# Rotary lanes 32 partitions apart, exchanged by ScalarE copies instead of permutation products

## The reference, cut to what matters

```
xr = x[..., :ROT_DIM]; x1, x2 = xr[..., :half], xr[..., half:]      # ROT_DIM 16, half 8
rot = concatenate([x1 * cos - x2 * sin, x2 * cos + x1 * sin])
x = concatenate([rot, x[..., ROT_DIM:]])
```

## Time and profile before

| | us |
|---|---|
| median of 3 runs | 2611.5 (2610.76 to 2611.63) |
| the profiled execution, its own time | 2610.73 |
| its span in the profile | 2608.9 |
| TensorE busy | 2572.1 (99%) |
| VectorE busy | 1674.5 (64%) |
| ScalarE busy | 1380.8 (53%) |
| granted TensorE clock, mean | 0.998 |

### The profile page before, as it was taken

How to read it: one execution, slowest core, us unless ns; L and a number is a source line. 1 busy time by engine, 2 the same in 40 slices (tenths; PEclk the granted TensorE clock), 3 DMA queues, 4 the chain that set the end, 5 groups by cost and what they waited for, 6 DMA issues and landing times.

```text
span 2608.9 us, 38082 instructions
## 1 busy us (share of the span) xinstructions
PE 2572.1 (99%) x14854; PEld 2228.0 (85%) x14854; DVE 1674.5 (64%) x1827; ACT 1380.8 (53%) x1640; POOL 61.1 (2%) x30
## 2 busy tenths in 40 slices
PE   8999999999999999999999999999999999999998
PEld 7888898888888988888888888888888888898887
DVE  7766687556765666666666666666766666665665
ACT  6644565445545664454455544544654454465544
POOL 0000000001000000000000000000000000000000
PEclk9999999999999999999999999999999999999999
DMA  7455534554554345555543455454345555543551
GB/s 272 144 196 191 181 138 178 193 191 173 196 192 178 130 148 191 193 177 193 193 146 117 176 192 193 178 193 177 130 154 193 185 185 186 186 161 114 194 193 65
DMA packets 63496, 454.36 MB, mean 174 GB/s; under 512 B 7088, under 2 KB 7344, under 8 KB 8992
## 3 DMA queue, kind: packets, MB, share of 16 engines
q1 hardware_dynamic: 62064, 449.15, 48.0%
q0 software_dynamic: 896, 3.05, 0.4%
q10 hardware_dynamic: 432, 0.68, 0.1%
HBM read 451.79 MB, written 1.05 MB: 174 GB/s over the span
## 4 chain that ended last, share of the span: by engine, by line
PE 92%; DVE 4%; ACT 3%; issue 1%; DMA 0%; ACTq 0%; DVEq 0%
PE tb L489 28%; PE tb L494 14%; PE acc L287 10%; PE acc L288 10%; PE acc L289 10%; PE acc L253 2%; PE acc L255 2%; PE acc L256 2%; PE acc L897 1%; DVE w_lo L211 1%; PE acc L489 1%; PE acc L899 1%; PE acc L898 1%; PE tb L318 1%; ACT w_hi L204 1%
## 5 line engine op out<-in xcount | busy, mean ns | idle before, releaser
L211 DVE TENSOR_TENSOR w_lo<-raw,w_hi 128x2048 fp32r<-128x2048 f32 x416 | 952.6, 2293 | 314.7 <-ACT w_hi L204 314.5
L204 ACT ACTIVATE w_hi<-raw 128x2048 fp32r<-128x2048 f32 x425 | 812.9, 1914 | 314.4 <-PE acc L289 276.5
L489 PE MATMUL tb<-xT,w_hi 128*128 128x512 f32 x3168 | 792.0, 392 | 0.0
L489 PEld LDWEIGHTS tb<-xT,w_hi 128*128 128x128 f32 x3168 | 576.3, 188 | 108.5 <-DVE big L682 0.2
L494 PEld LDWEIGHTS tb<-xT,w_lo 128*128 128x128 f32 x3168 | 432.1, 190 | 31.0
L494 PE MATMUL tb<-xT,w_lo 128*128 128x256 f32 x3168 | 441.7, 282 | 0.0
L287 PE MATMUL acc<-w_hi,cat 128*128 128x512 f32 x1024 | 402.8, 393 | 3.5 <-DVE cat L582 3.5
L288 PE MATMUL acc<-w_hi,cat 128*128 128x512 f32 x1024 | 399.9, 390 | 0.0
L289 PE MATMUL acc<-w_lo,cat 128*128 128x512 f32 x1024 | 398.7, 389 | 0.0
L287 PEld LDWEIGHTS acc<-w_hi,cat 128*128 128x128 f32 x1024 | 192.7, 188 | 42.8 <-DVE cat L582 3.9
L289 PEld LDWEIGHTS acc<-w_lo,cat 128*128 128x128 f32 x1024 | 192.3, 188 | 41.1
(11 more groups left out here) (349 smaller groups left out, 2882.7 us busy)
## 6 DMA issues: line engine op xcount, KB each, us to landing
raw<-in_stream SPq DMA_DIRECT2D x425, 1024.0 KB, 4.8
h<-in_x SPq DMA_DIRECT2D x2, 512.0 KB, 5.9
xn<-in_gates POOLq DMA_DIRECT2D x2, 512.0 KB, 8.0
gain<-in_gains POOLq DMA_DIRECT2D x2, 512.0 KB, 5.3
out<-xn SPq DMA_DIRECT2D x2, 512.0 KB, 2.9
cst<-in_consts SPq DMA_DIRECT2D x1, 832.0 KB, 12.6
raw<-in_stream ACTq DMA_DIRECT2D x1, 512.0 KB, 8.3
raw<-in_stream SPq DMA_DIRECT2D x1, 512.0 KB, 9.1
```

What stands on the lines that cost most here:

```text
L204: act.activation(w_hi[:, k % SPLIT, :], raw[:, k % RAW, :], ACT.Copy).then_inc(hi_done, 1)
L211: dve.tensor_tensor(w_lo[:, k % SPLIT, :], raw[:, k % RAW, :], w_hi[:, k % SPLIT, :], ALU.subtract).then_inc(lo_done, 1)
L489: return pe.matmul(bank, w_hi[:, c % SPLIT, at:at + P], xT[:, kt, :, :].rearrange("p a t -> p (a t)"), start=first, stop=last)
```

## The change

- The host reorders the columns of the q and k weights (`partners_apart`): in each 64 lanes the second eight rotary lanes change places with lanes 32 to 39. Partners then lie 32 partitions apart. The sign of the sine goes into the table rows.
- The matrix `rot` and its 16 products are gone. The constants' two DMAs are cut at the next boundary and carry 64 KB less in all.
- ScalarE does not copy the whole bank as it is, but with four activations of 32 partitions x 512 columns each, from partitions 32.. to 0.., 0.. to 32.., 96.. to 64.., 64.. to 96.. (`shift`), into one of two buffers `partner`, which lie in `gain`, not used at that time. Before it reuses a buffer it waits for `turned` of the tile that used it last.
- These copies stand behind the split of the same point of ScalarE's queue, not ahead of it. In `qkv_act` and `mix_a_act` the same change of order is made.
- VectorE multiplies the bank itself with the cosine, the partner buffer with the sine, and adds. It waits for `shifted`. In `qkv_dve` the split of chunk 4 moves between the two first turns.
- In `plan` the entries "rotate" are now "turn", so the cut in steps of 24 is unchanged; TensorE skips them.

```diff
-                        seq.append(("rotate", e - 1))
+                        seq.append(("turn", e - 1))
-            def rotate(self, e):
-                self.pe.wait_ge(*when("copied", (self.i, e)))
-                self.pe.matmul(fed_bank(e), rot, q_or_k(e), start=True, stop=True)\
-                    .then_inc(*sig("rotated", (self.i, e)))
...
                 for unit in units:
-                    {"product": self.product, "rotate": self.rotate, "block": self.block}[unit[0]](*unit[1:])
+                    if unit[0] != "turn":
+                        {"product": self.product, "block": self.block}[unit[0]](*unit[1:])
...
+        def shift(act, dst, bank, done):
+            for a in range(0, P, HD):
+                for to, of in ((a, a + HD // 2), (a + HD // 2, a)):
+                    last = act.activation(dst[to:to + HD // 2, :], bank[of:of + HD // 2, :], ACT.Copy)
+            last.then_inc(*sig("shifted", done))
...
-        def copy_act(act, i, c, e):
+        def shift_act(act, i, c, e):
             used(act, c + e)
-            act.activation(q_or_k(e), fed_bank(e), ACT.Copy).then_inc(*sig("copied", (i, e)))
+            if e >= 3:
+                act.wait_ge(*when("turned", (i, e - 3)))
+            shift(act, partner[e % 3], fed_bank(e), (i, e))
...
-            b, r = two(q_or_k(e)), two(rot_a)
+            b, r = two(q_or_k(e)), two(partner[e % 3])
-            dve.wait_ge(*when("rotated", (i, e)))
-            if e:
-                dve.wait_ge(*when("turned", (i, e - (1 if e % 3 == 1 else 2))))
-            dve.tensor_tensor(r, two(fed_bank(e)), sin, ALU.mult)
-            dve.tensor_tensor(b, b, cos, ALU.mult).then_inc(*sig("own", ("turn", i, e)))
+            dve.wait_ge(*when("shifted", (i, e)))
+            dve.tensor_tensor(b, two(fed_bank(e)), cos, ALU.mult)
+            dve.tensor_tensor(r, r, sin, ALU.mult).then_inc(*sig("own", ("turn", i, e)))
             dve.wait_ge(*when("own", ("turn", i, e)))
             dve.tensor_tensor(b, b, r, ALU.add).then_inc(*sig("turned", (i, e)))
...
                         v_take(act, i, c, unit[1])
-                    elif kind == "moba":
-                        copy_act(act, i, c, unit[1])
                     split_hi(act, c, unit[1] + SPLIT)
+                    if kind == "moba" and unit[1] % 3 != 2:
+                        shift_act(act, i, c, unit[1])
...
         def qkv_act(act, kind, i, c, n):
-            if kind == "moba":
-                copy_act(act, i, c, 0)
             split_hi(act, c, SPLIT)
             if kind == "moba":
-                copy_act(act, i, c, 1)
+                shift_act(act, i, c, 0)
             split_hi(act, c, 1 + SPLIT)
+            if kind == "moba":
+                shift_act(act, i, c, 1)
...
                 split_lo(dve, c, SPLIT)
-                turn_dve(dve, i, 0)
-                turn_dve(dve, i, 1)
+                turn_dve(dve, i, c, 0)
+                split_lo(dve, c, 1 + SPLIT)
+                turn_dve(dve, i, c, 1)
...
-            product(K0, {7: lambda: rotate(Q0)})
+            product(K0)
...
-            rotate(K0)
             product(G1)
...
-            product(K1, {3: lambda: rotate(Q1)})
-            value(V0, {4: lambda: rotate(K1)})
+            product(K1)
+            value(V0)
...
-            raw_copy(Q0)
             split_hi(act, c, Q0 + SPLIT)
-            raw_copy(K0)
+            apart(Q0)
             split_hi(act, c, K0 + SPLIT)
+            apart(K0)
...
-            raw_copy(Q1)
+            apart(Q1)
...
             exps(1)
-            raw_copy(K1)
+            apart(K1)
             split_hi(act, c, Q1 + SPLIT)
             flip_copy(0)
             split_hi(act, c, K1 + SPLIT)
             values(V0)
...
+def partners_apart(w):
+    at, half_ = np.arange(HD), HD // 8
+    at[half_:2 * half_], at[HD // 2:HD // 2 + half_] = at[HD // 2:HD // 2 + half_].copy(), at[half_:2 * half_].copy()
+    return w.reshape(w.shape[0], -1, HD)[:, :, at].reshape(w.shape)
```

More of the change, by code:

```diff
@@ L55 @@
 C_ID, C_FREQ = 0, P
-C_ROT, C_FOLD, C_TRI, C_ALL, C_STRICT, C_CAUSNEG, C_STRNEG = [P + 1 + i * P for i in range(7)]
-C_COSM, C_SINM, C_TURN, C_END = [8 * P + 1 + i * SEQ for i in range(4)]
+C_FOLD, C_TRI, C_ALL, C_STRICT, C_CAUSNEG, C_STRNEG = [P + 1 + i * P for i in range(6)]
+C_COSM, C_SINM, C_TURN, C_END = [7 * P + 1 + i * SEQ for i in range(4)]
 L_CONV, L_CONVB, L_BA, L_BX, L_LAM, L_SUB, L_END = 0, 16, 20, 24, 28, 32, 33
@@ L172, in write @@
         m_q, m_k, m_v = cut(0, HEADS, SEQ), cut(4096, HEADS, SEQ), cut(8192, TT, D)
-        rot_a = cut(9216, 512)
         p_in = cut(4096, 2, SEQ)
+        partner = [gain[:, 512 * j:512 * j + 512] for j in range(2)]
         m_pT = [cut(6144 + 2 * CAUSAL * i, 2, CAUSAL) for i in range(2)]
@@ L1041, in run @@
                 for unit in units:
-                    {"product": self.product, "rotate": self.rotate, "block": self.block}[unit[0]](*unit[1:])
+                    if unit[0] != "turn":
+                        {"product": self.product, "block": self.block}[unit[0]](*unit[1:])
             def begin(self, n):
-                turned = self.kind == "moba"
                 for u in range(UNITS):
@@ L1053, in begin @@
                 for u in range(UNITS):
-                    if turned and u in (4, 14):
-                        self.rotate(u // 14)
                     self.product(2, u)
@@ L1116, in feed_dve @@
                         split_lo(dve, c, unit[1] + SPLIT)
-                if unit[0] == "rotate":
-                    turn_dve(dve, i, unit[1])
+                if unit[0] == "turn":
+                    turn_dve(dve, i, c, unit[1])
                 if unit == ("block", 7):
@@ L1142, in qkv_dve @@
                 take_dve(dve, kind, i, c, n, 1)
-            split_lo(dve, c, 1 + SPLIT)
+                split_lo(dve, c, 1 + SPLIT)
             split_lo(dve, c, 2 + SPLIT)
@@ L1738, in value @@
                      view=half, between=between)
[L1740 to L1743, removed]
             def scores(hd):
@@ L1841, in mix_a_act, with apart @@
             par = lru_par[:, l, :]
-            def raw_copy(j):
+            def apart(j):
                 used(act, c + j)
-                act.activation(a_dst(j), two(A_BANK[j]), ACT.Copy).then_inc(*sig("a_raw", (l, j)))
+                if j in (Q1, K1):
+                    act.wait_ge(*when("turned", ("a", l, Q0 if j == Q1 else K0)))
+                shift(act, partner[j in (K0, K1)], A_BANK[j], ("a", l, j))
             def exps(hd):
@@ L1961, in turn @@
             def turn(j):
-                b, bank = a_dst(j), two(A_BANK[j])
-                dve.wait_ge(*when("rotated", ("a", l, j)))
-                dve.tensor_tensor(bank, bank, rb_sin.unsqueeze(1).to_broadcast([P, 2, SEQ]), ALU.mult)
-                dve.tensor_tensor(b, b, rb_cos.unsqueeze(1).to_broadcast([P, 2, SEQ]),
+                b, r = a_dst(j), two(partner[j in (K0, K1)])
+                dve.wait_ge(*when("shifted", ("a", l, j)))
+                dve.tensor_tensor(b, two(A_BANK[j]), rb_cos.unsqueeze(1).to_broadcast([P, 2, SEQ]), ALU.mult)
+                dve.tensor_tensor(r, r, rb_sin.unsqueeze(1).to_broadcast([P, 2, SEQ]),
                                   ALU.mult).then_inc(*sig("own", ("turn", "a", l, j)))
                 dve.wait_ge(*when("own", ("turn", "a", l, j)))
-                dve.tensor_tensor(b, b, bank, ALU.add).then_inc(*sig("turned", ("a", l, j)))
+                dve.tensor_tensor(b, b, r, ALU.add).then_inc(*sig("turned", ("a", l, j)))
             def conv(t):
@@ L2194, in _ @@
             load(1, 1)
-            sp.dma_start(cst[:, C_ROT:C_END], consts[:, C_ROT:C_END]).then_inc(*sig("const_in", 0, 16))
+            sp.dma_start(cst[:, C_FOLD:C_END], consts[:, C_FOLD:C_END]).then_inc(*sig("const_in", 0, 16))
             for k in range(2, RAW):
@@ L2348, in constants @@
     c[:, C_ID:C_ID + P] = k == m
-    half_ = HD // 8
-    for h0 in (0, HD):
-        for j in range(half_):
-            a = h0 + j
-            c[a + half_, C_ROT + a] = -1.0
-            c[a, C_ROT + a + half_] = 1.0
     c[:, C_FOLD:C_FOLD + P] = (k >= HD) & (m >= HD) & (k % MLA_ROPE == m % MLA_ROPE)
@@ L2408, in lay_stream @@
     for l in range(DEPTH_A):
-        q, k, v, xr, gr = (column_chunks(a["w_in"][l][:, 512 * j:512 * (j + 1)]) for j in range(5))
+        q, k, v, xr, gr = (a["w_in"][l][:, 512 * j:512 * (j + 1)] for j in range(5))
+        q, k, v, xr, gr = (column_chunks(w) for w in (partners_apart(q), partners_apart(k), v, xr, gr))
         out.extend(xr + [gr[0], q[0], k[0], gr[1], q[1], k[1]] + v)
@@ L2439, in lay_stream @@
             o = a["sb_w_o_2"][i // 3] if kind == "stick" else a["moba_w_o_2"][0]
-            q, k, v = (column_chunks(w[:, at:at + D]) for at in (0, D, 2 * D))
+            q, k, v = (w[:, at:at + D] for at in (0, D, 2 * D))
+            if kind == "moba":
+                q, k = partners_apart(q), partners_apart(k)
+            q, k, v = (column_chunks(part) for part in (q, k, v))
```

12 lines of the change are left out of this document (6 added, 6 removed).

## The result

| | before | after |
|---|---|---|
| median of 18 runs each, us | 2611.99 (2610.51 to 2612.89) | 2617.35 (2615.11 to 2620.92) |
| ratio | | 1.0021, 95% interval 1.0014 to 1.0028 |
| profiled execution, us | 2610.73 | 2618.12 |
| span, us; mean granted clock of TensorE | 2608.9; 0.998 | 2616.3; 0.994 |

The forecast was 2609.1 with a range up to 2612.6. The kernel became slower, by 5.4 us in the medians and 7.4 us in the profiled executions.

What follows compares the result with a forecast made beforehand. It took TensorE's chain (92%) as the bound, with gates waiting on VectorE and ScalarE deciding the gain. Profiled 2610.73 - 4.9 (moba) + 2.5 (mixers) = 2608.3, plus 0.8 to the median: 2609.1 us, range 2604.2 to 2612.6.

Steps and rivals of the forecast that it cites:

- The price of the copies: ScalarE: 0.60 us per 32-partition copy (0.49 to 0.69), four done after 2.4 us, queue going on after 2.3.
- Moba: Layer with block gates: gains 3.3 us ahead of the first gate and 1.6 over two laps, 4.9 in all.
- Laps: Moba, from gate to gate of TensorE: 25.0 us after the change, 25.8 before; two laps give 1.6.
- The first gate: Moba, product 6: starts at 1362.3 instead of 1365.58, 3.3 us earlier, with TensorE waiting about 1.7.
- the split of chunk 5: Moba, ScalarE ahead of the first gate: starts at 1339.8 instead of 1341.49, 1.70 us earlier.
- The mixers: Copies in ScalarE's dense stretch delay `head(0)` by 1.0 us in the first and 1.5 in the second, 2.5 lost.
- saving two rotations gives nothing: First mixer, scores of head 0: they already waited 0.48 us for the turned K0, with VectorE busy and unchanged.
- Behind `head(0)` TensorE runs without a stop and nothing is given back: Second mixer: the 1.5 us delay of `head(0)` stays as it is through the work behind it.
- TensorE's time is the time: Rival, whole kernel: all 16 rotations and their waits come out, 15.1 us, giving 2596.4; chance 0.09.
- Copies exceed what the gates give: Rival, ScalarE in mixers and moba's shifts: slower from 0.67 us per copy, 2612.3 at 0.69; chance 0.15.
- 2618 for 0.85 us a copy: Case of the slower rival: switching partitions drains ScalarE, each copy takes 0.85 us, the kernel 2618.
- within 0.2%: Whole kernel: time changes by less than 5.2 us either way, the measurement's limit; chance 0.67.

Runs made afterwards that it cites:

- e10: Changed kernel with one ScalarE copy of 128x512 in place of the four of 32x512, so partners are not exchanged: 2604.36 us, ratio 0.9967.
- e5: Changed kernel plus products nobody reads, filling TensorE's stalls in the mixers and ahead of moba's product 6, product 9 and scores of pair 6: 2612.57 us, ratio 1.0003.
- e4: Kernel before with the 16 rotation products left out and nothing in their place, tiles multiplied with themselves: 2608.63 us, ratio 0.9987.
- e6: Kernel before with the new rotation in moba only, ScalarE copying and VectorE turning ahead of their splits: 2605.55 us, ratio 0.9974.
- e8: Kernel before with eight idle ScalarE copies (4.8 us) ahead of K1's copy in each mixer, rotations kept: 2624.93 us, ratio 1.0048.
- e9: Kernel of e8 with four extra TensorE products of 0.85 us each directly ahead of K1's rotation, filling the stall: 2620.01 us, ratio 1.0031.
- e7: Changed kernel with e6's order in moba and another order of ScalarE's and VectorE's work in the mixers: 2607.93 us, ratio 0.9986.
- e11: e6 with Q0 and K0 of the mixers also rotated by copies, Q1 and K1 still by TensorE: 2606.90 us, ratio 0.9982.
- e1: Kernel before with the change's new rotation in moba only, mixers keeping old copies and rotations: 2611.36 us, ratio 0.9998.
- e2: Kernel before with the change's new rotation in the mixers only, moba keeping old copies and rotations: 2620.38 us, ratio 1.0028.

## Why the prediction was wrong

**The price of the copies** was right: 0.59 busy, 0.60 from start to start. The size of a copy's neighbours was not. The forecast let ScalarE's queue go on 2.3 us after the first copy. The rows show 2.42, and the copy follows a split at 1.93 (1340.13 to 1342.06), where splits were left after 1.80. A shift occupies 2.55 in all, 0.25 more than the sum took, because there is overlap neither between the copies nor to what stands on either side of them. In e10 one copy of 128x512 stands in the same place and follows the split at 1.80 (1345.52 to 1347.32), so the overlap is lost with the copies of 32 partitions or with their shifted start partitions, which no run separates. The Trainium skill's overlap of about 93 ns (ScalarE: Activation LUTs, What ACT_TABLE_LOAD costs), which the prediction weighed, is seen in no pair here that has one of the new copies in it.

**Moba.** Laps were forecast at 25.0 and the first measured 25.08. The second, 1397.27 to 1423.93, is 26.66, and the 1.6 more are the 3.4 us at half clock. The waits of 2.0, 1.9 and 1.9 were forecast as 1.7, 1.9 and 1.9. The first gate gained 2.8 us relative to the layer's entry, not 3.3: the split of chunk 5 was to start at 1339.8 and starts at 1349.58, or 1340.2 after taking off the 9.4 us by which the layer was late. That is 0.4 late, with two shifts ahead of it in the queue. Moba gained 2.7 us, not 4.9: 0.5 went at the first gate and 1.6 to the clock.

**The mixers.** The place was right: ScalarE without idle time from `exps(1)` to `values(V0)`, and `head(0)` late by its own wait for `values(V0)`. The first mixer's scores of head 0 wait 2.19 us instead of 0.48, which is the forecast's "saving two rotations gives nothing". `head(0)` was late by 1.4 us in the first mixer (1.84 less the 0.4 of its entry) and by 2.0 in the second (6.35 less 4.34), against 1.0 and 1.5. The difference of 0.4 and 0.5 is about what 0.25 us for each of two and three shifts gives (0.5 and 0.75).

**The step that failed** is the sentence "Behind `head(0)` TensorE runs without a stop and nothing is given back", and with it the sum, in which a stall costs its length. TensorE had waited 1.22 and 3.19 us for the turned K1 before `head(0)`, and then for `values(V0)`; these stalls are in the forecast, with no price beyond the delay. In them the clock fell to one half, and after `head(0)` had started 2.5 and 1.6 us more were lost. That term was put at nothing in both mixers and in moba. The sum by what was measured: -2.4 forecast, +0.9 for the mixers' larger delay (3.4 for 2.5), +0.6 for the first gate and the laps, +7.3 for the clock, 0.4 ahead of the first mixer and 0.6 at the end, 7.4; the profiled execution showed 7.4. Of the 7.3 for the clock 1.6 belong to the wait for `cat`, which is not of the change. Without any of it the sum is 0.1, no gain, where 2.4 were forecast; e5, whose products fill the stalls of `head(0)` and moba, measured 0.3 us slower.

**The rivals.** "Copies exceed what the gates give" had the right sign and place, and even 2618 for 0.85 us a copy. But its mechanism was a dearer copy, and the copies cost 0.60; that its number comes near is luck. "TensorE's time is the time" is refuted by e4: 3.5 us for all 16 rotations, where it says 15.1. The confidence in "within 0.2%", 0.67, came from treating the copy's price as the only unknown.

**What stays open.** Why a wait of 1.8 us at 448.6 was followed by half clock in this profiled run, and its twin of 1.74 us in the kernel before was not, no run separates. It is not the change: all thirteen traces have this wait twice, between 127 and 136 and between 435 and 454 us, and 11 of the 26 are followed by 3.4 us at half clock, e6's at 441.9 among them, whose mixers are those of before. Runs of one kernel differ in how many stretches fall: the changed kernel's lie between 2615.1 us at a mean clock of 0.996 and 2620.9 at 0.994. So a single trace prices a stretch, 1.6 us for 3.4 at half clock where nothing else waits, but not how often it comes.

## What to carry to other kernels

- When work is taken off TensorE, ask what it was covering. If the next gate waits for another engine, the product that goes is replaced by a stall, and the stall can cost more than half as much again in clock behind it (4.6 to 4.9 beside 8.0 us in e8 and e9). In e4's moba the loss is larger than the gain: eight products left out, 1.6 us slower.
- Price an added operation in the queue that carries it, with its borders, and look for stretches of that queue in which idle time is smaller than the sum of what is added. There neither another order nor a part of the change saved it (e7, e11); where such time is at hand, the order alone decided between nothing and the gain (e6: 5.8 us below e1).
- Look at the granted clock beside the waits whenever an expected loss is too small.

## What the runs showed of the hardware that was not expected

- TensorE's clock fell in the second of two stalls of only 1.2 and 1.7 us that lay 1.3 us apart (first mixer; e2 shows the same), and behind some single ones of 1.9 to 2.0 us at moba's gates, for 3.4 or 6.8 us. Over all thirteen traces from 20 us on: the single waits of 3.2 to 3.6 us (four) and of 2.4 to 2.6 us (three) all brought it down, those of 1.73 to 2.19 us, with the waits for `cat`, in 17 of 43 cases, those of 1.17 to 1.70 us, e10's gates among them, never. Products that nobody reads, 0.85 us each, in the stall's place kept it up.
- A ScalarE copy of 32x512 takes 589 ns, within 2% of one of 128x512 at 0.60. It is the columns that cost here, and four quarter-height copies take four times as long. From SBUF eight of them span 5.09 us (e8), 0.64 each.
